# Value sums of attention: the two halves added on VectorE and transposed, instead of one fp32 product with a stacked identity

## The chip, the cores and the metric

One core of a Trainium2 chip runs the whole program. The metric is the device time of one execution in microseconds. It has five engines that run side by side and wait for each other by semaphores: TensorE (PE; its weight loads are shown apart as PEld), VectorE (DVE), ScalarE (ACT), GpSimd (POOL) and SyncE (SP, which issues the DMAs).

## The reference, cut to what matters

The reference is a two-layer diffusion backbone over 1024 latent and 256 context tokens. The change lies in the attention of each layer, which has 10 heads (4 latent-attention heads of key width 96, "MLA"; 6 grouped-query heads of width 64, "GQA"), all with values of width 64:

```python
def block(qi):
    s = jnp.einsum('bkgqd,bksd->bkgqs', qi, k).astype(F32) * scale
    p = jax.nn.softmax(s, axis=-1).astype(v.dtype)
    return jnp.einsum('bkgqs,bkse->bkgqe', p, v)
```

Latent queries see all 1280 keys. In layer 0 the 256 context queries are computed too, and see the 256 context keys only; layer 1 computes latent queries alone.

## The kernel before, in words

Everything is fp32. To multiply faster, an operand is split into a high part (`pth` of the probabilities) that the fast fp32r product takes exactly, and the remainder (`ptl`). The values stand the same way: the stationary tile of a value product (`mvs`, `gvs`) is 128 columns wide, 64 columns of the high part and 64 of the low part. The value sum `O` therefore comes out as two halves, 64 partitions each, that have to be added, and it is feature by token, while the normalisation by the softmax sum wants token by feature.

Work is cut into turns n, one block of 128 queries of one head each: N = 100 in layer 0 (8 latent blocks and then 2 context blocks per head) and N = 80 in layer 1. Two turns make a pair G = n // 2, whose value products go to one PSUM bank `O[G % 2]`. Pairs: 50 in layer 0 and 40 in layer 1. No scheduler is at work: each engine has its instructions in the order in which the code writes them, and waits in that order.

In turn n, PE does this (the loop at L1252): `transposes(n)` of the probabilities into the scores' bank (L1207); in an even turn the high value product of pair n/2 - 1 (L1233), in an odd turn the low one; in an even turn `fold_halves` of pair n/2 - 2 (L1243); then `scores(n + 2)` (L1195), in pieces, each of which waits until `low(n)` on VectorE has read the same piece of the bank (`lo_done`).

VectorE in turn n (L1389): `maximum(n + 1)` (L1345, L1348), `low(n)` (three subtractions, L1363, then one reciprocal, L1367), `first_part(n + 2)`, the maximum over the first 512 scores (L1337), and in an even turn `normalise` of pair n/2 - 2 (L1377).

ScalarE: `high(n)` (L1309), a flush now and then (L1285), `exp(n + 1)` (L1298), and in an odd turn `evacuate` (L1291), which copies the 128 x 256 value sum of pair n // 2 - 1 from PSUM to `osb`.

`fold_halves` multiplies `osb` by `fold`, two 64 x 64 identities on top of each other. This adds the halves and turns them to token by feature in one step. It is an ordinary fp32 product, 2 instructions per pair; the profile lists 2 records for each.

`flush(n)` on PE puts two transposes of finished output (L1218) before the last two blocks of `transposes(n)`, in 5 (layer 0) or 4 (layer 1) successive turns after every second head; 2 of them are even turns.

Of the kernel before, what the change touches and what calls it, by code (L numbers as in the profile page):

```python
# [15 lines left out]
P = 128  # L16
# [34 lines left out]
def backbone(nc, a):  # L51
# [970 lines left out]
    def attention(layer, last, first_head, unit, early, block, ret):  # L1022
# [14 lines left out]
        with Scope() as s:  # L1037
# [9 lines left out]
            negmax, rsum = s.sb("negmax", [P, N]), s.sb("rsum", [P, N])  # L1047
            part_max, rinv = s.sb("part_max", [P, N, 2]), s.sb("rinv", [P, N])
            osb = [s.sb(f"osb{i}", [P, 256]) for i in range(2)]
            fold = s.sb("fold", [P, HD])  # L1050
            o_tok = s.sb("o_tok", [P, BLK, P])
            o_feat = s.sb("o_feat", [P, 2, 256])
            S = [s.ps(f"scores{i}", [P, 3 * 512]) for i in range(2)]
# [3 lines left out]
            s_first, part_done, rest_done = s.sem("s_first"), s.sem("part_done"), s.sem("rest_done")  # L1057
            s_done, max_done, exp_done = s.sem("s_done"), s.sem("max_done"), s.sem("exp_done")
            t_done, hi_done, lo_done = s.sem("t_done"), s.sem("hi_done"), s.sem("lo_done")
            pv_done, osb_done, fold_done, o_done = s.sem("pv_done"), s.sem("osb_done"), s.sem("fold_done"), s.sem("o_done")  # L1060
            own, folder = s.sem("own"), s.sem("folder")
            flush_t, flushed = s.sem("flush_t"), s.sem("flushed")
            stored = [s.sem(f"stored{i}") for i in range(2)]
            early_in, early_hi, early_lo = s.sem("early_in"), s.sem("early_hi"), s.sem("early_lo")
# [108 lines left out]
            def _(pe):  # L1173
# [61 lines left out]
                    if end:  # L1235
                        mm.then_inc(pv_done, 1)

                def fold_halves(G):
                    pe.wait_ge(osb_done, G + 1)
                    if G == 0:  # L1240
                        pe.wait_ge(folder, 1)
                    for j in range(2):
                        mm = nc.tensor.matmul(O[G % 2][:, 256 + j * HD:256 + (j + 1) * HD], osb[G % 2][:, j * P:(j + 1) * P], fold[:, :],  # L1243
                                              start=True, stop=True)
                    mm.then_inc(fold_done, 1)
                scores(0)
                ret.variance(pe, ret.turns - 2)
                ret.outer(pe, ret.turns - 1)
# [3 lines left out]
                for n in range(N + FLUSH0 + NP):  # L1252
                    if n == 0:
                        scores(2)
                        continue
                    if n < N:
                        transposes(n)
                    elif flush_of(n):
                        flush(n)
                    G = n // 2 - 1  # L1260
                    if 0 <= G < NG:
                        if n % 2 == 0:
                            if G >= 2:
                                pe.wait_ge(o_done, G - 1)
                            values(G, pth, hi_done, cut[2 * G + 2], False)
                        else:
                            values(G, ptl, lo_done, cut[2 * G + 2], True)
                    if n % 2 == 0 and 0 <= G - 1 < NG:
                        fold_halves(G - 1)
                    if n + 2 < N:  # L1270
                        scores(n + 2)

# [14 lines left out]
            def evacuate(act, G):  # L1287
                act.wait_ge(pv_done, G + 1)
                if G >= 2:
                    act.wait_ge(fold_done, G - 1)  # L1290
                nc.scalar.activation(osb[G % 2][:, :], O[G % 2][:, :256], ACT.Copy).then_inc(osb_done, 1)  # L1291

            @block.scalar
            def _(act):
# [38 lines left out]
            def _(dve):  # L1333
# [16 lines left out]
                def low(n):  # L1350
                    G, j = n // 2, n % 2
                    if j == 0 and G >= 2:
                        dve.wait_ge(pv_done, G - 1)
                    if n == 2:
                        dve.wait_ge(ret.out_done, ret.turns)
                        for k in range(2):
                            dve.wait_ge(ret.out_stored[k], 16 * (ret.turns // 2))
                    for p, (k0, k1) in enumerate(pieces(n)):
                        dve.wait_ge(hi_done, cut[n] + p + 1)
                        if k0 == 8 and flush_of(n):  # L1360
                            g, f = flush_of(n)
                            dve.wait_ge(flushed, g * NP + f + 1)
                        nc.vector.tensor_tensor(ptl[G % 2][:, k0:k1, j * P:(j + 1) * P],  # L1363
                                                S[n % 2][:, k0 * P:k1 * P].rearrange("p (b q) -> p b q", q=P),
                                                pth[G % 2][:, k0:k1, j * P:(j + 1) * P].bitcast(f32), ALU.subtract).then_inc(lo_done, 1)
                    dve.wait_ge(exp_done, n + 1)
                    nc.vector.reciprocal(rinv[:, n:n + 1], rsum[:, n:n + 1]).then_inc(own, 1)  # L1367

                def normalise(G):
                    n = 2 * G  # L1370
                    g, hd, f = n // NS, head_of(n) % 2, (n % NH) // 2
                    b = block_of(n)
                    dve.wait_ge(fold_done, G + 1)
                    dve.wait_ge(own, n + 2)
                    if g:
                        dve.wait_ge(flush_t, (g - 1) * NP + f + 1)
                    nc.vector.tensor_tensor(o_tok[:, b:b + 2, hd * HD:(hd + 1) * HD],  # L1377
                                            O[G % 2][:, 256:256 + 2 * HD].rearrange("p (j e) -> p j e", e=HD),
                                            rinv[:, n:n + 2].unsqueeze(2).to_broadcast([P, 2, HD]), ALU.mult).then_inc(o_done, 1)
                first_part(0)  # L1380
                maximum(0)
# [2 lines left out]
                first_part(1)  # L1384
                maximum(1)
                ret.finish(dve, ret.turns - 1)
                nc.vector.tensor_tensor(fold[:, :], ident[:, :HD], ident[:, HD:], ALU.add).then_inc(folder, 1)
                first_part(2)
                for n in range(1, N + FLUSH0 + NP):  # L1389
                    if n + 1 < N:  # L1390
                        maximum(n + 1)
                    if n < N:
                        low(n)
                    if n + 2 < N:
                        first_part(n + 2)
                    if n % 2 == 0 and 0 <= n // 2 - 2 < NG:
# [1126 lines left out]
```

## Time and profile before

| what | value |
|---|---|
| median of 3 runs | 3383.92 us (3383.41 to 3385.73) |
| the profiled execution's own time | 3385.56 us |
| its span | 3383.8 us |
| PE busy | 3321.8 us, 98% of the span |
| DVE busy | 2246.2 us, 66% |
| ACT busy | 1252.0 us, 37% |
| attention, layer 0 | about 454 to 827 us of the span |
| attention, layer 1 | about 2228 to 2549 us |

The busy share of an engine counts its instructions, not how well they fill it. Within attention the engines wait for each other inside every turn, so a share over the whole span says little about it; the order of starts in the timeline does.

### The profile page before, as it was taken

To read this page: it belongs to the slowest core of one execution; us is meant where nothing else is said; L and a number is where in the kernel's file an instruction comes from. 1 tells how busy PE (TensorE), PEld (TensorE's weight loads), DVE (VectorE), ACT (ScalarE), POOL (GpSimd) and SP (SyncE) were. 2 spreads that over 40 slices of the span, in tenths; PEclk is the share of its full clock that TensorE was granted. 3 is DMA by queue.
4 is the path that set the end of the run, shared out by engine and by line. 5 is a ranking of instruction groups with operands and counts; after the bars stand their busy time and mean duration, and the time that the engine had idled before them with its cause. 6 is when DMAs were issued, how large, how long until landed. Compare 5 with 4: busy or idle time off the path is not lost. (4 is left out here: it accounts for less than half of the span.)

```text
span 3383.8 us, 48755 instructions
## 1 busy us (share of the span) xinstructions
PE 3321.8 (98%) x17988; PEld 2825.5 (84%) x17988; DVE 2246.2 (66%) x3432; ACT 1252.0 (37%) x2128; POOL 1068.4 (32%) x1121
## 2 busy tenths in 40 slices
PE   8999999999999999999999999999999999999998
PEld 4888888888888888888888788889998788888886
DVE  6575567887178888888756543578992656656566
ACT  4332356776241122112223432366772322222222
POOL 0222310111424444444434122410014344343443
PEclk9999999999999999999999999999999999999999
DMA  6445562222112222222110424462212111111111
GB/s 255 151 184 213 148 197 64 54 71 71 40 56 75 74 74 74 74 80 75 54 39 26 180 103 153 145 199 53 58 43 89 38 55 44 50 50 43 50 44 61
DMA packets 100272, 305.34 MB, mean 90 GB/s; under 512 B 12448, under 2 KB 39200, under 8 KB 97824
## 3 DMA queue, kind: packets, MB, share of 16 engines
q1 hardware_dynamic: 100128, 303.40, 27.6%
q8 instruction: 93, 1.52, 0.2%
q14 instruction: 51, 0.42, 0.0%
HBM read 240.17 MB, written 63.18 MB: 90 GB/s over the span
## 5 line engine op out<-in xcount | busy, mean ns | idle before, releaser
L131 POOL TENSOR_TENSOR wlo<-raw,whi 128x256 fp32r<-128x256 f32 x516 | 494.6, 988 | 814.9 <-ACT whi L119 814.9
L2270 DVE SCALAR_TENSOR_TENSOR xT<-down_acc,mod,xT 128x512 f32<-128x512 f32 (+1 forms) x800 | 496.3, 694 | 236.1 <-PE down_acc L194 234.1
L1993 POOL TENSOR_TENSOR hid_lo<-y,hid_hi 128x256 fp32r<-128x256 f32 (+1 forms) x189 | 185.2, 1011 | 622.5 <-ACT hid_hi L2167 622.5
L2156 ACT ACTIVATE up<-up_acc 128x512 f32<-128x512 f32 (+1 forms) x210 | 115.4, 551 | 580.0 <-PE up_acc L194 579.0
L192 PE MATMUL up_acc<-mix_hi,whi 128*128 128x512 f32 (+1 forms) x875 | 323.6, 370 | 1.8 <-DVE mix_lo L487 0.9
L193 PE MATMUL up_acc<-mix_lo,whi 128*128 128x512 f32 (+1 forms) x875 | 322.5, 369 | 0.0
L194 PE MATMUL up_acc<-mix_hi,wlo 128*128 128x512 f32 (+1 forms) x875 | 322.0, 368 | 0.0
L192 PE MATMUL up_acc<-late_hi,whi 128*128 128x512 f32 (+1 forms) x860 | 316.7, 368 | 0.0
L194 PE MATMUL up_acc<-late_hi,wlo 128*128 128x512 f32 (+1 forms) x860 | 316.4, 368 | 0.0
L193 PE MATMUL up_acc<-late_lo,whi 128*128 128x512 f32 (+1 forms) x860 | 316.4, 368 | 0.0
L192 PE MATMUL down_acc<-hid_hi,first_whi 128*128 128x512 f32 (+1 forms) x825 | 304.6, 369 | 1.4 <-DVE xT L2317 1.4
L193 PE MATMUL down_acc<-hid_lo,first_whi 128*128 128x512 f32 (+1 forms) x825 | 303.3, 368 | 0.0
L194 PE MATMUL down_acc<-hid_hi,first_wlo 128*128 128x512 f32 (+1 forms) x825 | 303.3, 368 | 0.0
L1309 ACT ACTIVATE pth<-scores 128x512 fp32r<-128x512 f32 (+1 forms) x500 | 225.8, 522 | 189.8 <-PE scores L1207 189.8
L1363 DVE TENSOR_TENSOR ptl<-scores,pth 128x512 fp32r<-128x512 f32 (+1 forms) x500 | 267.0, 587 | 20.3 <-ACT pth L1309 19.8
L247 DVE CUSTOM_DVE_ANT_0 mod_product<-norm_buf,silu_all 128x1024 f32<-128x1024 f32 x156 | 234.8, 1505 | 20.4 <-DMA norm_buf<-in_w_ada 11.0
L131 POOL TENSOR_TENSOR first_wlo<-first_raw,first_whi 128x256 fp32r<-128x256 f32 x220 | 210.2, 986 | 113.3 <-ACT first_whi L119 113.3
L119 ACT ACTIVATE first_whi<-first_raw 128x1024 fp32r<-128x1024 f32 x55 | 58.3, 1060 | 465.5 <-PE down_acc L194 391.8
L1298 ACT ACTIVATE probs<-scores,negmax 128x1280 f32<-128x1280 f32 (+1 forms) x180 | 224.7, 1248 | 10.1 <-DVE negmax L1348 10.1
L1207 PE MATMUL scores<-ident,probs 128*128 128x128 f32 x1640 | 216.9, 274 | 5.3 <-ACT probs L1298 5.3
L2249 DVE TENSOR_SCALAR y<-up,convw 128x1284 f32<-128x1284 f32 (+1 forms) x86 | 92.3, 1073 | 189.9 <-ACT up L2156 180.4
L1207 PEld LDWEIGHTS scores<-ident,probs 128*128 128x128 f32 x1640 | 184.7, 141 | 8.4 <-ACT probs L1298 7.8
(329 smaller groups left out, 7501.7 us busy)
## 6 DMA issues: line engine op xcount, KB each, us to landing
raw<-in_w_rest SPq DMA_DIRECT2D x112, 512.0 KB, 3.6
norm_buf<-in_w_ada SPq DMA_DIRECT2D x78, 512.0 KB, 4.5
first_raw<-in_w_rest SPq DMA_DIRECT2D x57, 512.0 KB, 3.6
proj_scratch<-stage SPq DMA_DIRECT2D x18, 640.0 KB, 4.4
raw<-in_w_first SPq DMA_DIRECT2D x21, 512.0 KB, 6.7
ada_raw<-in_w_ada SPq DMA_DIRECT2D x6, 1536.0 KB, 14.5
xT<-proj_scratch SPq DMA_DIRECT2D x4, 1920.0 KB, 8.9
xT<-in_xT SPq DMA_DIRECT2D x8, 640.0 KB, 24.9
```

What stands on the lines that cost most here:

```text
L131: m = nc.gpsimd.tensor_tensor(self.lo[k][:, x:x + 256], self.raw[k][:, x:x + 256], self.hi[k][:, x:x + 256].bitcast(f32), ALU.subtract)
L192: nc.tensor.matmul(out, hi, xhi, start=start, stop=False)
L193: nc.tensor.matmul(out, hi, xlo, start=False, stop=False)
L194: return nc.tensor.matmul(out, lo, xhi, start=False, stop=stop)
L247: nc.vector.tensor_tensor_reduce(product[:, :], self.raw[:, f, :], silu_all[:, :, w], 1.0, 0.0, ALU.mult, ALU.add, self.sums[:, f, w:w + 1 ...
L1207: tr = nc.tensor.transpose(S[n % 2][:, b * P:(b + 1) * P], probs[n % 2][:, b * P:(b + 1) * P], ident[:, :])
L1298: nc.scalar.activation(probs[n % 2][:, :nk], S[n % 2][:, :nk], ACT.Exp, bias=negmax[:, n:n + 1], accum_out=rsum[:, n:n + 1]).then_inc(exp_ ...
L1309: nc.scalar.activation(pth[G % 2][:, k0:k1, j * P:(j + 1) * P], S[n % 2][:, k0 * P:k1 * P].rearrange("p (b q) -> p b q", q=P), ACT.Copy).t ...
L1363: nc.vector.tensor_tensor(ptl[G % 2][:, k0:k1, j * P:(j + 1) * P], S[n % 2][:, k0 * P:k1 * P].rearrange("p (b q) -> p b q", q=P), pth[G % ...
L1993: m = nc.gpsimd.tensor_tensor(hid_lo[:, x:z], y[1][:, x:z], hid_hi[:, x:z].bitcast(f32), ALU.subtract)
L2156: nc.scalar.activation(up[half][:, pc:pc + w], ub[c][:, :w], ACT.Copy).then_inc(up_evac, 1)
L2270: nc.vector.scalar_tensor_tensor(xs, db[g % DB][:, :w], mod_of(layer, 5, m, c), xs, ALU.mult, ALU.add).then_inc(added, 1)
```

## The change

- `evacuate` on ScalarE copies only the lower half (partitions 64 to 127) of the sum, to `lows`, which is 64 partitions of an existing tile (`product`).
- New on VectorE: `add_halves(G)` adds the upper half in PSUM and `lows`, 64 x 256, into `osb`. Its place is behind `low(n)` of the even turn n = 2G + 4, ahead of `first_part(n + 2)`.
- `to_tokens` on PE replaces `fold_halves` at the same place: two 128 x 128 transposes of `osb` with the identity. It waits for `sum_done` from VectorE where `fold_halves` waited for `osb_done` from ScalarE.
- The reciprocals are taken for two blocks at once, in odd turns only.
- Two clearings of the unused half of `osb` replace the addition that made `fold`, once per layer.

```diff
-                def fold_halves(G):
-                    pe.wait_ge(osb_done, G + 1)
+                def to_tokens(G):
+                    pe.wait_ge(sum_done, G + 1)
                     if G == 0:
-                        pe.wait_ge(folder, 1)
+                        pe.wait_ge(zeroed, 1)
                     for j in range(2):
-                        mm = nc.tensor.matmul(O[G % 2][:, 256 + j * HD:256 + (j + 1) * HD], osb[G % 2][:, j * P:(j + 1) * P], fold[:, :],
-                                              start=True, stop=True)
-                    mm.then_inc(fold_done, 1)
+                        tr = nc.tensor.transpose(O[G % 2][:, 256 + j * P:256 + (j + 1) * P], osb[G % 2][:, j * P:(j + 1) * P], ident[:, :])
+                    tr.then_inc(fold_done, 1)
...
-                        fold_halves(G - 1)
+                        to_tokens(G - 1)
...
             def evacuate(act, G):
                 act.wait_ge(pv_done, G + 1)
                 if G >= 2:
-                    act.wait_ge(fold_done, G - 1)
-                nc.scalar.activation(osb[G % 2][:, :], O[G % 2][:, :256], ACT.Copy).then_inc(osb_done, 1)
+                    act.wait_ge(sum_done, G - 1)
+                nc.scalar.activation(lows[G % 2], O[G % 2][HD:, :256], ACT.Copy).then_inc(low_out, 1)
...
-                    dve.wait_ge(exp_done, n + 1)
-                    nc.vector.reciprocal(rinv[:, n:n + 1], rsum[:, n:n + 1]).then_inc(own, 1)
+                    if j == 1:
+                        dve.wait_ge(exp_done, n + 1)
+                        nc.vector.reciprocal(rinv[:, n - 1:n + 1], rsum[:, n - 1:n + 1]).then_inc(own, 1)
+
+                def add_halves(G):
+                    dve.wait_ge(low_out, G + 1)
+                    if G >= 2:
+                        dve.wait_ge(fold_done, G - 1)
+                    nc.vector.tensor_tensor(osb[G % 2][:HD, :], O[G % 2][:HD, :256], lows[G % 2], ALU.add).then_inc(sum_done, 1)
...
                     if n < N:
                         low(n)
+                    if n % 2 == 0 and 0 <= n // 2 - 2 < NG:
+                        add_halves(n // 2 - 2)
                     if n + 2 < N:
                         first_part(n + 2)
```

The order of instructions at the first pair, with what each waits for. On VectorE, even turn 4 of layer 0, before: the three subtractions of `low`, the reciprocal, then the first part of the maximum of turn 6.

```order
L1363 TENSOR_TENSOR ptl_209<-scores_223,pth_210 128x4x128 [waits hi_done_241,pv_done_243]
L1363 TENSOR_TENSOR ptl_209<-scores_223,pth_210 128x4x128 [waits hi_done_241]
L1363 TENSOR_TENSOR ptl_209<-scores_223,pth_210 128x2x128 [waits hi_done_241]
L1367 RECIPROCAL rinv<-rsum 128x1 [waits exp_done_239]
L1337 TENSOR_REDUCE part_max<-scores_223 128x1 [waits s_first_234]
```

The same place now:

```order
L1362 TENSOR_TENSOR ptl_209<-scores_222,pth_210 128x4x128 [waits hi_done_240,pv_done_242]
L1362 TENSOR_TENSOR ptl_209<-scores_222,pth_210 128x4x128 [waits hi_done_240]
L1362 TENSOR_TENSOR ptl_209<-scores_222,pth_210 128x2x128 [waits hi_done_240]
L1373 TENSOR_TENSOR osb_218<-values_224,mod_product 64x256 [waits low_out_243]
L1336 TENSOR_REDUCE part_max<-scores_222 128x1 [waits s_first_233]
```

The addition of 64 x 256 has taken the reciprocal's place, and stands behind all three subtractions of the turn.

On PE, the same even turn before: the transposes of turn 4, the high value product of pair 1, the fold of pair 0, the first scores of turn 6.

```order
L1207 MATMUL scores_223<-ident,probs_212 128x128 [waits exp_done_239]
L1207 MATMUL scores_223<-ident,probs_212 128x128 x9
L1233 MATMUL values_226<-pth_208,mix_hi 128x256 [waits hi_done_241]
L1233 MATMUL values_226<-pth_208,mix_hi 128x256 x9
L1243 MATMUL values_225<-fold,osb_218 128x64 [waits folder_248,osb_done_244]
L1243 MATMUL values_225<-fold,osb_218 128x64
L1195 MATMUL scores_223<-first_kh,first_qh 128x512 [waits lo_done_242]
```

And now:

```order
L1207 MATMUL scores_222<-ident,probs_212 128x128 [waits exp_done_238]
L1207 MATMUL scores_222<-ident,probs_212 128x128 x9
L1233 MATMUL values_225<-pth_208,mix_hi 128x256 [waits hi_done_240]
L1233 MATMUL values_225<-pth_208,mix_hi 128x256 x9
L1243 MATMUL values_224<-ident,osb_218 128x128 [waits zeroed_248,sum_done_244]
L1243 MATMUL values_224<-ident,osb_218 128x128
L1195 MATMUL scores_222<-first_kh,first_qh 128x512 [waits lo_done_241]
```

Nothing has moved on PE. The instruction ahead of the scores now waits for VectorE's `sum_done`, which comes from the addition shown above, instead of ScalarE's `osb_done`.

## Rows read from the trace of the kernel before

**Rows 1.** Page, part 1: busy time, share and instructions of each engine.

```profile
PE 3321.8 (98%) x17988; PEld 2825.5 (84%) x17988; DVE 2246.2 (66%) x3432; ACT 1252.0 (37%) x2128; POOL 1068.4 (32%) x1121
```

**Rows 2.** Groups by shape, DVE, 454 to 830 us: busy us, mean ns, idle before.

```profile
L1363 DVE TENSOR_TENSOR ptl<-scores,pth 128x256 fp32r<-128x256 f32 x100 | 41.5, 415 | 3.7 <-ACT pth L1309 3.7
L1377 DVE TENSOR_TENSOR o_tok<-values,rinv 128x128 f32<-128x128 f32 x50 | 14.0, 281 | 3.1 <-PE values L1243 3.1
```

**Rows 3.** Timeline, layer 1, GQA, even turn: start, duration us, [idle before, releaser].

```profile
2401.57 0.40 ACT L1291 ACTIVATE osb<-values 128x256 f32<-128x256 f32 x1
...
2401.98 1.25 PE L1207 MATMUL scores<-ident,probs 128*128 128x128 f32 x10
...
2403.38 1.62 DVE L1363 TENSOR_TENSOR ptl<-scores,pth 128x512 fp32r<-128x512 f32 x3
...
2404.14 0.53 PEld L1243 LDWEIGHTS values<-fold,osb 128*128 128x128 f32 x4
...
2404.59 0.19 PEld L1195 LDWEIGHTS scores<-ks,qh 128*128 128x128 f32 x1
...
2404.91 0.15 DVE L1367 RECIPROCAL rinv<-rsum 128x1 f32<-128x1 f32 x1
...
2405.37 0.69 DVE L1337 TENSOR_REDUCE part_max<-scores 128x1 f32<-128x512 f32 x1 [0.30 <-PE scores L1195]
```

**Rows 4.** Timeline, layer 0, MLA, even turn with full blocks on both sides.

```profile
513.60 0.30 PEld L1195 LDWEIGHTS scores<-mix_lo,qh 96*128 96x128 f32 x2
...
513.92 0.15 DVE L1367 RECIPROCAL rinv<-rsum 128x1 f32<-128x1 f32 x1
```

**Rows 5.** Timeline, layer 0, MLA, even turn that begins a head.

```profile
505.22 0.30 PEld L1195 LDWEIGHTS scores<-mix_lo,qh 96*128 96x128 f32 x2 [0.40 <-DVE ptl L1363]
...
506.01 0.15 DVE L1367 RECIPROCAL rinv<-rsum 128x1 f32<-128x1 f32 x1
```

**Rows 6.** Timeline, layer 0, GQA, even turn that begins a head.

```profile
655.04 1.62 DVE L1363 TENSOR_TENSOR ptl<-scores,pth 128x512 fp32r<-128x512 f32 x3
...
655.78 0.19 PEld L1195 LDWEIGHTS scores<-ks,qh 128*128 128x128 f32 x1 [0.40 <-DVE ptl L1363]
...
656.58 0.15 DVE L1367 RECIPROCAL rinv<-rsum 128x1 f32<-128x1 f32 x1
```

**Rows 7.** Timeline, layer 0, MLA, last full even turn of a head, context next.

```profile
492.33 0.19 PEld L1195 LDWEIGHTS scores<-first_kh,first_qh 96*128 96x128 f32 x1
...
492.64 0.15 DVE L1367 RECIPROCAL rinv<-rsum 128x1 f32<-128x1 f32 x1
...
493.12 1.07 PEld L1207 LDWEIGHTS scores<-ident,probs 128*128 128x128 f32 x10 [0.37 <-ACT probs L1298]
```

**Rows 8.** Timeline, layer 0, MLA, even context turn.

```profile
497.13 0.15 DVE L1367 RECIPROCAL rinv<-rsum 128x1 f32<-128x1 f32 x1
...
497.56 0.30 PEld L1195 LDWEIGHTS scores<-mix_lo,qh 96*128 96x128 f32 x2
```

**Rows 9.** Timeline, layer 0, GQA: the two transposes of a flush.

```profile
633.84 0.25 PEld L1218 LDWEIGHTS scores<-ident,o_tok 128*128 128x128 f32 x2
```

**Rows 10.** Who waited, line 1195's scores for `ptl`: us in total, times.

```profile
PEld scores L1195: 28.5, 65
```

**Rows 11.** Busy by window: length, PE, PEld, DVE, ACT, POOL, granted clock, DMA, GB/s.

```profile
468.00:471.40 3.40, 3.23 (x9) 2.65 (x10) 1.80 (x5) 1.35 (x3) 0.00 (x0) 0.51 0.99 351
```

**Rows 12.** Timeline of PE alone, third turn of layer 0, and of layer 1.

```profile
465.99 1.31 PE L1207 MATMUL scores<-ident,probs 128*128 128x128 f32 x10 [1.03 <-ACT probs L1298]
468.17 0.80 PE L1195 MATMUL scores<-first_kh,first_qh 96*128 96x512 f32 x1 [0.87 <-DVE ptl L1363]
...
475.42 0.40 PE L1195 MATMUL scores<-first_kh,first_qh 96*128 96x512 f32 x1
...
479.45 0.40 PE L1195 MATMUL scores<-first_kh,first_qh 96*128 96x512 f32 x1
...
2235.29 0.50 PE L1195 MATMUL scores<-first_kh,first_qh 96*128 96x512 f32 x1 [0.86 <-DVE ptl L1363]
```

More of the change, by code:

```diff
@@ L1049, in attention @@
             osb = [s.sb(f"osb{i}", [P, 256]) for i in range(2)]
-            fold = s.sb("fold", [P, HD])
+            lows = [product[0:HD, i * 256:(i + 1) * 256] for i in range(2)]
             o_tok = s.sb("o_tok", [P, BLK, P])
@@ L1059, in attention @@
             t_done, hi_done, lo_done = s.sem("t_done"), s.sem("hi_done"), s.sem("lo_done")
-            pv_done, osb_done, fold_done, o_done = s.sem("pv_done"), s.sem("osb_done"), s.sem("fold_done"), s.sem("o_done")
-            own, folder = s.sem("own"), s.sem("folder")
+            pv_done, low_out, sum_done, fold_done, o_done = (s.sem(x) for x in ("pv_done", "low_out", "sum_done", "fold_done", "o_done"))
+            own, zeroed = s.sem("own"), s.sem("zeroed")
             flush_t, flushed = s.sem("flush_t"), s.sem("flushed")
@@ L1373, in normalise @@
                     dve.wait_ge(fold_done, G + 1)
-                    dve.wait_ge(own, n + 2)
+                    dve.wait_ge(own, G + 1)
                     if g:
@@ L1377, in normalise @@
                     nc.vector.tensor_tensor(o_tok[:, b:b + 2, hd * HD:(hd + 1) * HD],
-                                            O[G % 2][:, 256:256 + 2 * HD].rearrange("p (j e) -> p j e", e=HD),
+                                            O[G % 2][:, 256:].rearrange("p (j e) -> p j e", e=P)[:, :, :HD],
                                             rinv[:, n:n + 2].unsqueeze(2).to_broadcast([P, 2, HD]), ALU.mult).then_inc(o_done, 1)
@@ L1386, in _ @@
                 ret.finish(dve, ret.turns - 1)
-                nc.vector.tensor_tensor(fold[:, :], ident[:, :HD], ident[:, HD:], ALU.add).then_inc(folder, 1)
+                for b in osb:
+                    zero = nc.vector.memset(b[HD:, :], 0.0)
+                zero.then_inc(zeroed, 1)
                 first_part(2)
```

## The prediction

> **What bounds the kernel now.** I read the page first: PE is busy for 98% of the span [rows 1], so time is either PE's own work or a wait put in front of it. The fold is PE work, and lies in attention alone, so the rest of the reading is the timeline there, one pair at a time.
>
> Take an even turn of layer 1 [rows 3]. PE transposes (2401.98), makes the high value product, loads for the fold (2404.14), and goes straight on to the next scores (2404.59). The fold costs PE 0.45 us, and waits for nothing: the copy to `osb` had ended at 2401.97, over 2 us before. VectorE runs the three subtractions of `low` from 2403.38; the reciprocal's start at 2404.91 marks their end. What the reader is to see is that PE begins the next scores 0.32 us before VectorE has finished `low`. That is allowed because scores go piece by piece behind it. VectorE's next maximum then sits idle for 0.30 us until PE's scores are there. So in an even turn PE is ahead, and VectorE follows it.
>
> **The change part by part.** *PE.* The fold's 0.45 us go. Two transposes of 128 x 128 come. The two of a flush show a load time of 0.25 us for two loads of 0.14 us [rows 9], so they start 0.11 us apart and PE is through with two in some 0.21 us. Saved: 0.24 us per pair, over 90 pairs 22 us, if nothing else moved.
>
> The Trainium skill (Perfetto Trace Analysis, Transposes) says to do logical transposes in transpose mode and not as a standard matmul. The trace agrees on PE's own price, 0.21 against 0.45 us; by that rule alone the sum would be -22 us. It does not speak of what the transposes have to wait for.
>
> *VectorE.* The addition of 64 x 256 with one operand in PSUM has no row. The nearest is the 128 x 256 subtraction with one operand in PSUM, 0.415 us [rows 2]; the columns are the same, and I take 0.42. From below it is bounded by the 128-column multiplication from PSUM, 0.28 us [rows 2], from above by the 512-column reduction, 0.69 us [rows 3]. The even turn's reciprocal, 0.15 us, goes; the addition starts in its place. In odd turns the reciprocal of two columns costs what that of one did.
>
> *ScalarE.* Copying 64 partitions instead of 128 with the same columns stays at some 0.40 us [rows 3]; that copy ends far ahead either way. If it got slower by a microsecond it would still be hidden behind `high` and `exp`. The two clearings and the missing `fold` are a few tenths per layer, behind the first turns.
>
> *The wait that is added.* This is the main term. `to_tokens` waits for the addition, which stands behind all of `low(n)` of the same even turn. Behind `to_tokens` on PE are queued the scores of turn n + 2, then everything. So these scores lose their piecewise start: they can begin only at the time where the reciprocal started, plus 0.42 (addition), plus 0.05 (from VectorE's end to PE's load, read where the first subtraction, 655.04 and 0.69 long, released the load at 655.78 [rows 6]), plus 0.21 (transposes), in all 0.68 us after the row of the reciprocal. Applied place by place:
>
> - Full blocks on both sides. GQA: 2404.91 + 0.68 = 2405.59 against 2404.59 [rows 3], +1.00. MLA: 513.92 + 0.68 = 514.60 against 513.60 [rows 4], +1.00. In turns with a flush PE reaches the place 0.22 us later anyway [rows 9] and `low` does not, so +0.78. Layer 0 has 19 such pairs (4 with a flush), layer 1 has 37 (8 with a flush). Without flush 44 x 1.00 = 44.0; with it 12 x 0.78 = 9.4.
> - The even turn that begins a head in layer 0, 9 times. The value product is of a context pair and short, so PE is early and waited for the first piece already. 506.01 + 0.68 = 506.69 against 505.22 [rows 5], +1.47; GQA 656.58 + 0.68 = 657.26 against 655.78 [rows 6], +1.48. 9 x 1.47 = 13.2.
> - The last full even turn of a head, 10 times. The scores are of a context block and short, and PE then waited 0.37 us for the exponential [rows 7]. The scores took from 492.33 to 493.12 - 0.37 = 492.75, so 0.42. Now 492.64 + 0.68 + 0.42 = 493.74 against 493.12, +0.62; with a flush (4) +0.40. Sum 5.3.
> - The even context turn, 9 times with scores behind it: 497.13 + 0.68 = 497.81 against 497.56 [rows 8], +0.25. Sum 2.3.
> - First and last pairs of both layers, where no scores follow: some 0.5 in all.
>
> Does a later wait swallow the shift? The transposes of turn n + 1 follow the scores on PE directly. VectorE's maximum of turn n + 2 already waited for those scores [rows 3], so it moves by the same amount, and `low(n + 1)` with it. The waits of the odd turns hang on a chain that itself starts at the shifted scores, so I let nothing be swallowed. DMAs are far ahead and get more time.
>
> Sum: 44.0 + 9.4 + 13.2 + 5.3 + 2.3 + 0.5 = 74.7 us. This is made on the profiled execution, span 3383.8 (own time 3385.56, inside the spread of the three runs); the median is 3383.92. Forecast 3383.9 + 74.7 = 3458.6 us, slower by 2.2%.
>
> **The rivals.** *The clock falls as well.* In the third turn of layer 0 PE ran nothing but ten transposes from 464.96 (465.99 less its idle 1.03) to 468.17 [rows 12]; the granted clock in the window behind it was 0.51, the 1.2 GHz level [rows 11]. From these scores to the next took 7.25 us, where the full clock gave 4.03 (475.42 to 479.45) [rows 12]: a fall costs 3.2 us. The same gap in layer 1 (scores at 2235.29 after the same waits) did not make it fall. With the change the beginning of a head looks alike: ten transposes, two short value products, and 2 us of waiting. If the clock falls at all 9, the time is 3458.6 + 29 = 3487 us. For it: one of two such gaps fell. Against it: here a little real work lies inside. Chance 0.2, and a fall at all the other pairs too (56 x 3.2 = 179 more, near 3670 us) 0.03; there a whole high value product of ten matmuls lies between.
> The Trainium skill (TensorE: Matmul & The Clock Gate, Part 4: PE-mode transpose) says that transposes do not count as PE being busy for the clock. By that rule, the gap of layer 0 [rows 12], filled with transposes alone, agrees; the like gap in layer 1 passed at full clock and does not bear it out.
>
> *The shift is partly swallowed.* PE waited for `ptl` ahead of scores 65 times, 28.5 us in all [rows 10]. If the shifts used all of it up, the sum is 74.7 - 28.5 = 46 us, 3430 us. Against it is the argument above. Chance 0.08.
>
> *The other side: PE's saving shows and the addition is hidden.* VectorE would have to hand over the sum before PE has ended its high value product; the point where this decides is `low` ending 0.47 us before PE arrives. Then the time is 3383.9 - 22 = 3362 us. The skill's rule on transposes named above gives this. Against it: the subtractions end 0.77 us after PE gets there (2404.91 against 2404.14) [rows 3]. Chance 0.03. That the two effects meet within measurement: 0.02.
>
> **How the numbers follow.** Forecast 0.64, clock at the heads' beginnings 0.2, clock everywhere 0.03, swallowed 0.08, faster 0.03, none 0.02. The unknown duration of the addition acts on about 84 places: at 0.28 us the sum falls by 12 (3447), at 0.69 us it rises by 23 (3481). The likeliest case's own range is 3446 to 3475; with the clock's rival above the range is 3444 to 3488 us. A measurement of this kernel tells 0.2% (7 us) from no change; faster has 0.03, the same 0.02, slower 0.95.
>
> **What would show it.** In the profile after: `to_tokens` (L1243) released by VectorE's `osb` addition at nearly every pair, with a wait of about 0.8 us; its two transposes 0.11 us apart; the addition at 0.42 us, starting where the reciprocal did; the idle of VectorE before the first maximum (L1336) of even turns as before or longer; the distance from one even turn to the next grown by 1.0 us; attention longer by some 39 us in layer 0 and 36 in layer 1, all else unmoved; and the clock near 1.00 except where a head begins, if the rival holds. The forecast is wrong if the pair's period grows by much less than a microsecond although the wait is there: then something on the chain had slack that I did not see. It is wrong upward if the clock's row shows half speed inside attention.

## The result and the profile after

The changed kernel takes 3462.21 us (median of 4 runs, 3459.87 to 3466.85) against 3383.66 us (4 runs, 3383.28 to 3385.73) for the kernel before on the same chip: the ratio is 1.0233, with an interval of 1.0215 to 1.025. It is slower by 78.6 us, where 74.7 us were forecast. The profiled execution took 3459.87 us with a span of 3458.0 us; against the span before of 3383.8 us that is 74.2 us more.

The page's first part, which answers to [rows 1]:

```profile
PE 3320.4 (96%) x17808; PEld 2809.1 (81%) x17808; DVE 2273.3 (66%) x3434; ACT 1260.4 (36%) x2128; POOL 1071.5 (31%) x1121
```

PE does 1.4 us less work than before in a span 74 us longer, so nearly all of the loss is time in which PE stands idle. Where it stands is in the view of line 1243 (durations in ns, then the idle time before it in us and how often):

```profile
L1243 PEld LDWEIGHTS values<-ident,osb x180: 137/141/145, 481.1 to 2621.5; 128*128 128x128 f32 x180
L1243 PE MATMUL values<-ident,osb x180: 271/273/332, 481.1 to 2621.6; 128*128 128x128 f32 x180
...
  DVE osb L1373: 184.1, 178
```

The 184.1 us count two rows for each wait. The view of who waited for whom keeps the loads and the matmuls apart (total us, times, longest us); below its first line stand the two other waits around it:

```profile
PEld values L1243 <- DVE osb L1373: 101.1, 89, 2.1
DVE part_max L1336 <- PE scores L1195: 94.0, 106, 1.8
...
PEld scores L1195 <- DVE ptl L1362: 23.1, 51, 1.7
```

Before the change the fold waited for VectorE nowhere. Now 89 of 90 pairs wait, for 101.1 / 89 = 1.14 us on average. VectorE in turn waits longer at its next maximum (94.0 us, where the same view of before has 49.9), because PE's scores come later, and the scores' own wait for `ptl` falls only from 28.5 us [rows 10] to 23.1.

The timeline of the turn of [rows 3], now 58 us later:

```profile
2459.36 0.38 ACT L1290 ACTIVATE mod_product<-values 64x256 f32<-64x256 f32 x1
...
2459.60 1.25 PE L1207 MATMUL scores<-ident,probs 128*128 128x128 f32 x10
...
2461.00 1.62 DVE L1362 TENSOR_TENSOR ptl<-scores,pth 128x512 fp32r<-128x512 f32 x3
...
2462.53 0.41 DVE L1373 TENSOR_TENSOR osb<-values,mod_product 64x256 f32<-64x256 f32 x1
...
2462.99 0.20 PEld L1243 LDWEIGHTS values<-ident,osb 128*128 128x128 f32 x2 [1.15 <-DVE osb L1373]
...
2463.16 0.19 PEld L1195 LDWEIGHTS scores<-ks,qh 128*128 128x128 f32 x1
...
2463.93 0.69 DVE L1336 TENSOR_REDUCE part_max<-scores 128x1 f32<-128x512 f32 x1 [0.99 <-PE scores L1195]
```

ScalarE's copy of the lower half has ended at 2459.74, and the sums of the upper half are there as long. The addition starts only at 2462.53, behind the three subtractions of a later turn. PE's loads have run out at about 2461.84 (2462.99 - 1.15), its matmuls 0.2 us later, and PE stands until the addition has ended. From the transposes of `probs` to the next scores it is 3.56 us (2459.60 to 2463.16), before it was 2.61 us (2401.98 to 2404.59) [rows 3]: 0.95 us lost in this pair.

At the beginning of a head in layer 0 the wait is the longest. The turn of [rows 5]:

```profile
501.23 1.25 PE L1207 MATMUL scores<-ident,probs 128*128 128x128 f32 x10
...
502.24 0.48 PE L1233 MATMUL values<-pth,mix_hi 128*128 128x256 f32 x2
...
504.17 0.41 DVE L1373 TENSOR_TENSOR osb<-values,mod_product 64x256 f32<-64x256 f32 x1
...
504.62 0.20 PEld L1243 LDWEIGHTS values<-ident,osb 128*128 128x128 f32 x2 [2.11 <-DVE osb L1373]
504.79 0.30 PEld L1195 LDWEIGHTS scores<-mix_lo,qh 96*128 96x128 f32 x2
```

PE's idle of 2.11 us is followed by a fall of the granted clock, that is a stretch of some microseconds at the lower of its two levels. Busy time by window behind four heads' beginnings (length, PE, PEld, DVE, ACT, POOL, granted clock, DMA share, GB/s):

```profile
504.00:508.00 4.00, 3.37 (x15) 3.04 (x16) 2.07 (x5) 0.59 (x2) 0.00 (x0) 0.75 0.93 210
592.00:596.00 4.00, 4.00 (x20) 3.44 (x18) 2.15 (x5) 0.79 (x2) 0.00 (x0) 0.65 0.02 4
673.00:677.00 4.00, 4.00 (x19) 3.65 (x18) 2.53 (x5) 0.90 (x2) 1.79 (x2) 0.57 0.32 125
752.00:756.00 4.00, 4.00 (x18) 3.60 (x17) 3.36 (x9) 2.27 (x4) 1.84 (x2) 0.60 0.31 127
```

The granted clock 0.57 in a window means that most of it ran at the 1.2 GHz level. PE looks fully busy there and did less: the last three windows hold 18 to 20 of its matmuls, and those of before at about the same times (592:596, 672:676, 752:756) 29 to 32. Before, the clock was 1.00 at all nine places where a head begins. In this execution it fell at four of them.

### The profile page after: what moved, and what is told of

Read it like the earlier page. It is cut to its first block and busy times, and to the rows that moved or that the text cites. A ratio compares the mean times of both kernels' runs of the same rounds, so it can differ in the third digit from the quotient of the medians.

```text
span 3458.0 us, 48483 instructions
## 1 busy us (share of the span) xinstructions
PE 3320.4 (96%) x17808; PEld 2809.1 (81%) x17808; DVE 2273.3 (66%) x3434; ACT 1260.4 (36%) x2128; POOL 1071.5 (31%) x1121
## 5 line engine op out<-in xcount | busy, mean ns | idle before, releaser
L192 PEld LDWEIGHTS up_acc<-mix_hi,whi 128*128 128x128 f32 x875 | 165.0, 189 | 31.9 <-issue 3.3
```

The costliest lines, as they stand in the source:

```text
L192: nc.tensor.matmul(out, hi, xhi, start=start, stop=False)
```

## The experiments

Each kernel was timed beside the kernel before. That one measured 3383.05 us in the company of the first four experiments, 3383.18 us with the next four, and 3383.6 us with the last two; each time its runs lay within 3382.2 and 3386. "Per pair" is the growth of the distance from the transposes of one even turn to those of the next turn, read in the two traces; where the odd turn behind it changes too, that is said.

**1. The addition ahead of the subtractions.** If the wait comes from the addition's place on VectorE, moving it by one call takes the loss away.

```
-                    if n < N:
-                        low(n)
                     if n % 2 == 0 and 0 <= n // 2 - 2 < NG:
                         add_halves(n // 2 - 2)
+                    if n < N:
+                        low(n)
```

> One line moved on VectorE against the changed kernel: the addition of the halves stands ahead of the even turn's three subtractions instead of behind them; everything it adds is still there. If the place of the addition in VectorE's order, with PE's scores queued behind the transposes, is the cause (my theory), PE finds the sum ready when its high value product ends, the wait of about 0.8 us per pair goes, and only the subtractions start 0.35 us later: nearly all of the 78 us go, and with the cheaper PE part the time is 3370 to 3385 us. If the added VectorE work itself is the cost (rival: VectorE is the bound, 0.25 us more per pair), at least 20 us stay wherever it stands: 3405 us or more. If the clock's falls are the main cost, the time follows them: they would go too only if PE's waits go.

Measured: 3379.62 us (3377.65 to 3380.37), ratio 0.9989 (0.998 to 0.9999). The whole 79 us are gone, with the same instructions in another order. Its timeline in layer 1:

```profile
2399.56 0.42 DVE L1373 TENSOR_TENSOR osb<-values,mod_product 64x256 f32<-64x256 f32 x1
2399.90 1.60 DVE L1362 TENSOR_TENSOR ptl<-scores,pth 128x512 fp32r<-128x512 f32 x3
...
2400.38 0.24 PEld L1243 LDWEIGHTS values<-ident,osb 128*128 128x128 f32 x2
...
2400.63 0.19 PEld L1195 LDWEIGHTS scores<-ks,qh 128*128 128x128 f32 x1
...
2401.22 0.19 PEld L1195 LDWEIGHTS scores<-ks,qh 128*128 128x128 f32 x1 [0.30 <-DVE ptl L1362]
```

The transposes wait for nothing. The subtractions start after the addition, and PE's second piece of scores waits for them (0.30 us): what is saved on PE is given back here. Per pair of full blocks MLA gains 0.11 to 0.25 us, mostly 0.17. GQA gains 0.05 in the even turn and 0.10 in the odd one behind it, and 0.23 where a flush lies. The beginning of a head loses 0.30, but for the second (0.04 gained). So VectorE's 0.41 us cost something in this place too, but far less.

**2. The transposes behind the scores.** The same knot, untied from the other side: the addition stays where it is, and PE does the next scores first.

```
-                    if n % 2 == 0 and 0 <= G - 1 < NG:
-                        to_tokens(G - 1)
                     if n + 2 < N:
                         scores(n + 2)
+                    if n % 2 == 0 and 0 <= G - 1 < NG:
+                        to_tokens(G - 1)
```

> One line moved on PE against the changed kernel: the two transposes of the summed halves stand behind the scores of turn n + 2 instead of ahead of them; VectorE's order is that of the changed kernel. If the cost is what is queued behind PE's wait (my theory), it goes although the addition still stands behind the subtractions: 3375 to 3395 us, a little above the experiment with the addition moved, since the normalisation now waits for PE's scores and delays VectorE's next maximum by some 0.1 to 0.3 us in the GQA heads. If the added VectorE work is the cost, 3405 us or more.

Measured: 3388.76 us (3386.0 to 3390.61), ratio 1.0015 (1.0005 to 1.0024). Of the 79 us 5.7 are left, although the addition is still behind `low`. The wait thus costs only through what is queued behind it on PE. What is left does not lie in the even turns of full blocks, which gain 0.12 to 0.24 us each but for two. VectorE's normalisation now waits for the transposes:

```profile
DVE o_tok L1383 <- PE values L1243: 24.4, 54, 0.6
```

The odd turns behind lose some 0.10 us each (4.7 in all) and the beginnings of a head 3.2 us together, and a fall of the clock at the start of layer 1 (behind 2241 us) takes another 1.6.

**3. The transposes alone.** The kernel before, with the product by `fold` replaced by transposes of the whole `osb`; there is no addition, so the low halves are left out of the result. The normalisation reads the columns where they now stand.

```
-                        mm = nc.tensor.matmul(O[G % 2][:, 256 + j * HD:256 + (j + 1) * HD], osb[G % 2][:, j * P:(j + 1) * P], fold[:, :],
-                                              start=True, stop=True)
+                        mm = nc.tensor.transpose(O[G % 2][:, 256 + j * P:256 + (j + 1) * P], osb[G % 2][:, j * P:(j + 1) * P], ident[:, :])
```

> The PE part alone, on the kernel before: ScalarE still copies all 128 partitions, PE transposes them in transpose mode instead of the product with the stacked identity, nothing is added on VectorE (the low halves are left out of the output), and PE waits for ScalarE as before. If the transposes save PE 0.24 us per pair as the rows say and PE's order carries it on, the time falls by up to 22 us in the MLA heads and less in the GQA heads where VectorE sets the pace: 3362 to 3376 us. If two transposes cost PE as much as the product (rival), 3383 us; slower than 3390 us would mean that the transposes themselves hurt, by the clock for example.

Measured: 3367.09 us (3366.7 to 3367.57), ratio 0.9952 (0.9935 to 0.9969). PE's saving is real: 0.22 to 0.24 us per pair of full blocks, MLA and GQA alike, and as much in the context turns. It is 0 where a head begins and in the last full turn, where PE was waiting anyway. That makes some 65 x 0.23 = 15 us. The profiled execution is 18.1 us shorter than the one before the change; the other 3.1 us are a fall of the clock in the first turns of layer 0 [rows 12] that it does not have. The rule of the Trainium skill (Perfetto Trace Analysis, Transposes) to use transpose mode for a logical transpose agrees with this run.

**4. The addition alone.** The changed kernel, with an fp32 product by the identity's first 64 columns in place of the transposes; the normalisation reads its columns accordingly.

```
-                        tr = nc.tensor.transpose(O[G % 2][:, 256 + j * P:256 + (j + 1) * P], osb[G % 2][:, j * P:(j + 1) * P], ident[:, :])
+                        tr = nc.tensor.matmul(O[G % 2][:, 256 + j * HD:256 + (j + 1) * HD], osb[G % 2][:, j * P:(j + 1) * P], ident[:, :HD],
+                                              start=True, stop=True)
```

> The addition alone, on the changed kernel: everything as changed, but the summed halves are turned to tokens by a fp32 product with 64 columns of the identity, as costly on PE as the one before. If the wait is the cost, the changed kernel's time plus 0.24 us for each of about 84 pairs whose scores are behind it: 3462 + 20 = 3482 us (3475 to 3488). If the transposes had a part in the loss, it is below 3462 us. The clock may help here: ordinary products stand where transposes stood, so fewer falls than 5 in attention if transposes do not count for it.

Measured: 3491.04 us (3489.81 to 3492.86), ratio 1.0318 (1.03 to 1.0335), above the upper end expected. Per pair it loses 1.22 us, 0.27 more than the changed kernel, as it should. With the last full turns, the context turns and the beginnings of a head that makes 23 of the 33 us between the two profiled executions. Most of the rest is the clock. It fell at six beginnings of a head, where the changed kernel's profile has four (3.0 us more), and in the first turns of layer 0 and of layer 1 (behind 468 and 2294 us), where that one has none (3.0 us each). Both have one more just behind layer 0's attention (884 and 864 us). Three of the six:

```profile
642.00:646.00 4.00, 4.00 (x19) 3.63 (x19) 2.00 (x4) 0.51 (x1) 0.00 (x0) 0.57 0.00 0
...
724.00:728.00 4.00, 4.00 (x17) 3.61 (x18) 1.77 (x3) 0.10 (x1) 0.00 (x0) 0.57 0.02 6
806.00:810.00 4.00, 4.00 (x18) 3.56 (x16) 3.38 (x7) 1.95 (x4) 0.00 (x0) 0.57 0.02 4
```

**5. The addition twice.** If `to_tokens` hangs on VectorE's chain alone, one more addition ahead of it moves every pair by its duration.

```
+                    nc.vector.tensor_tensor(product[0:HD, 512 + G % 2 * 256:768 + G % 2 * 256], O[G % 2][:HD, :256], lows[G % 2], ALU.add)
                     nc.vector.tensor_tensor(osb[G % 2][:HD, :], O[G % 2][:HD, :256], lows[G % 2], ALU.add).then_inc(sum_done, 1)
```

> The changed kernel with the addition made twice on VectorE in the same place (the first into columns that nobody reads). If every tenth of a microsecond in front of to_tokens goes straight into the period (my theory), each of some 88 places gets 0.35 us more: 3462 + 31 = 3493 us (3487 to 3500). If something later in the turn has slack, clearly less.

Measured: 3495.22 us (2 runs, 3491.69 and 3498.75), ratio 1.0331 (1.0312 to 1.035).

```profile
2487.80 0.41 DVE L1373 TENSOR_TENSOR mod_product<-values,mod_product 64x256 f32<-64x256 f32 x1
2488.13 0.41 DVE L1374 TENSOR_TENSOR osb<-values,mod_product 64x256 f32<-64x256 f32 x1
```

The two start 0.33 us apart, and the pairs' loss goes from 0.95 to 1.28 us, by just as much. No slack lies on the chain. In this run too the clock fell behind some beginnings of a head (640, 681, 722 and 804 us).

**6. GpSimd adds.** ScalarE copies both halves, and GpSimd, which had room, adds them in SBUF between its own splits. VectorE is rid of the addition.

```
+                nc.scalar.activation(ups[G % 2], O[G % 2][:HD, :256], ACT.Copy).then_inc(low_out, 1)
...
+                for G in range(NG):
+                    pool.wait_ge(low_out, 2 * G + 2)
...
+                    nc.gpsimd.tensor_tensor(osb[G % 2][:HD, :], ups[G % 2], lows[G % 2], ALU.add).then_inc(sum_done, 1)
+                    for _ in range(2):
+                        if steps and (steps[0][0] <= G):
+                            _, f, args = steps.pop(0)
+                            f(*args)
```

> The changed kernel with the addition taken off VectorE: ScalarE copies both halves out of PSUM (two copies of 64 x 256, 0.4 us more per pair, in time in which it waited for PE), GpSimd adds them in SBUF (64 x 256, about 1 us, interleaved with the splits that it makes in the later heads), PE transposes as changed and waits for GpSimd, and no instruction of VectorE stands in front. By my theory the sum is ready before PE asks for it, nothing waits, and PE's saving of 0.22 us per pair is all that is left: as with the transposes alone, 3364 to 3373 us, faster than both kernels. If the wait only changes its name (rival: GpSimd comes later than the high value product ends), 3390 us or more.

Measured: 3378.08 us (3375.49 to 3383.71), ratio 0.9984 (0.9975 to 0.9994): the best that computes everything, but 5 us above the range expected.

```profile
2398.81 0.38 ACT L1312 ACTIVATE mod_product<-values 64x256 f32<-64x256 f32 x1
...
2399.22 0.38 ACT L1313 ACTIVATE mod_product<-values 64x256 f32<-64x256 f32 x1
...
2399.67 0.72 POOL L1186 TENSOR_TENSOR osb<-mod_product 64x256 f32<-64x256 f32 x1 [4.72 <-ACT mod_product L1313]
...
2401.23 0.24 PEld L1265 LDWEIGHTS values<-ident,osb 128*128 128x128 f32 x2
```

GpSimd's sum is there at 2400.39, PE wants it at 2401.23. Full pairs gain 0.22 us as in experiment 3. What is missing lies elsewhere. The two profiled executions are 12.8 us apart. Of these, 8.4 us lie where the clock fell and did not in experiment 3: in the first turns of layer 0 (behind 469 us, 3.7), between the layers (823 us, 2.5) and in the first turns of layer 1 (2237 us, 2.2). The first and the last of these hold 0.6 us each that is not the clock's but belongs to the two clearings (see the terms of the sum below). The context turns are 2.0 us longer, where most of the waits for GpSimd lie (8.6 us in 16 turns in all), and the end of layer 1 is 1.9 us longer, with PE's wait of 1.66 us for GpSimd's last sum.

**7. PE filled at the heads' beginnings.** Ten idle matmuls of 256 columns behind the short context product, in layer 0 only, into a part of PSUM that the transposes overwrite. They lie inside the wait, so they cost nothing, unless the falls of the clock come from PE's idle time; then they save those.

```
                             values(G, pth, hi_done, cut[2 * G + 2], False)
+                            if is_ctx(2 * G) and n < N:
+                                h = head_of(2 * G)
+                                for k in range(10):
+                                    nc.tensor.matmul(O[G % 2][:, 256:], mvs[:, k % 2, h, :] if is_mla(h) else gvs[:, k % 2, h % 2, :],
+                                                     pth[G % 2][:, k % 2, :], start=False, stop=False)
```

> The changed kernel with ten more matmuls of 256 columns on PE in the even turn that begins a head in layer 0 (behind the two of the context pair, into columns of the bank that the transposes overwrite later), in the time in which PE waits for the sum. They take about 1.27 us of a wait of 1.9 us and delay nothing. If the clock's falls in the changed kernel (5 in layer 0's attention, 3.4 us each) come from that gap, they become rarer or stop, and each is worth 1.3 us: 3452 to 3459 us with a granted clock above that of the changed kernel. If the falls have nothing to do with it: 3462 us and as many falls.

Measured: 3458.32 us (3457.64 to 3460.29), ratio 1.0223 (1.0207 to 1.0238), 3.9 us below the changed kernel, whose runs were on another chip. The ten matmuls cost nothing: a head's beginning takes as long as in the changed kernel where the clock held.

**8. The wait alone.** The kernel before, with its product by `fold`, made to wait for `low(n)` of the same turn; no addition and no transposes.

```
                     if n % 2 == 0 and 0 <= G - 1 < NG:
+                        if n < N:
+                            pe.wait_ge(lo_done, cut[n + 1])
                         fold_halves(G - 1)
```

> The kernel before with one wait more and nothing else: PE waits for the last subtraction of the even turn ahead of the fold. No addition, the fp32 product and the copy on ScalarE as before. If the order is the cost and not the work, most of the loss is there without any addition: the scores start at the reciprocal's row plus 0.57 us (0.07 to the end of the subtractions, 0.05, the fold's 0.45) instead of 0.68, so about 0.89 us per full pair, 65 us in all and 3440 to 3458 us. If the addition's work is the cost, 3384 us.

Measured: 3450.66 us (2 runs, 3450.39 and 3450.93), ratio 1.0199 (1.018 to 1.0218): 67 us, without any of the change's arithmetic. The timeline:

```profile
2453.25 1.62 DVE L1365 TENSOR_TENSOR ptl<-scores,pth 128x512 fp32r<-128x512 f32 x3
...
2454.79 0.15 DVE L1369 RECIPROCAL rinv<-rsum 128x1 f32<-128x1 f32 x1
2454.92 0.52 PEld L1243 LDWEIGHTS values<-fold,osb 128*128 128x128 f32 x4 [0.84 <-DVE ptl L1365]
...
2455.36 0.19 PEld L1195 LDWEIGHTS scores<-ks,qh 128*128 128x128 f32 x1
```

**9 and 10. The changed kernel and the filled one, side by side.** The changed kernel had not been timed beside the filled one, and 3.9 us is little against its spread. So both ran again together, unaltered.

> The changed kernel unaltered, beside the filled one on the same chip: 3458 to 3466 us, with 2 to 6 falls of the clock in attention, at the beginnings of heads in layer 0.

> The filled kernel again on the same chip. If the ten matmuls at each head's beginning keep the clock up, no fall at those places and 3 to 7 us less than the changed kernel beside it; if the first look was chance, the two agree and falls are there.

Measured: the changed kernel 3465.62 us (3460.4 to 3467.12), the filled one 3456.41 us (3455.05 to 3457.98), 9.2 us less, where 3 to 7 were expected; the ranges do not touch. Windows of the changed kernel, behind three heads' beginnings:

```profile
508.00:512.00 4.00, 4.00 (x19) 3.67 (x18) 2.23 (x5) 0.72 (x2) 0.00 (x0) 0.57 1.01 227
552.00:556.00 4.00, 4.00 (x19) 3.88 (x18) 3.03 (x6) 1.57 (x4) 0.00 (x0) 0.57 0.00 0
675.00:679.00 4.00, 4.00 (x19) 3.66 (x19) 2.35 (x5) 0.73 (x2) 0.53 (x1) 0.57 0.53 164
```

And of the filled one, where in this run and in that of experiment 7 the clock fell at none of the nine beginnings:

```profile
508.00:512.00 4.00, 3.42 (x23) 2.95 (x22) 3.32 (x7) 2.10 (x4) 0.00 (x0) 1.00 0.95 228
592.00:596.00 4.00, 3.46 (x23) 3.05 (x23) 2.50 (x7) 1.30 (x4) 0.00 (x0) 1.00 0.00 0
672.00:676.00 4.00, 2.94 (x20) 2.55 (x20) 2.89 (x7) 1.89 (x5) 0.04 (x1) 1.00 0.49 168
```

The two profiled executions are 5.6 us apart: 4.5 at the beginnings of a head, and 1.3 between the layers, where the changed kernel has a fall at 867 us, just behind attention, that the filled one lacks. Whether the filling has a part in that one is open; in experiment 7 the clock fell there (860 us). The executions that make the rest of the 9.2 us have no profile.

## Why the prediction was right, step by step

**The wait is the cost, and its place on VectorE the cause.** This was the main term, and the runs show it from four sides: the wait alone gives 67 us (experiment 8), moving the addition ahead of `low` gives them back (1), moving the transposes out from in front of the scores does too (2), and a second addition adds its own 0.33 us to each pair (5). Predicted was that the scores load 0.68 us after the place of the reciprocal. It is 0.63 (2462.53 to 2463.16): the addition 0.41 instead of 0.42, the hand-over 0.05 as read, and the two transposes 0.17 (2462.99 to 2463.16) instead of 0.21. One of the signs was misjudged: the wait was put at about 0.8 us and is 1.15, near what the forecast's own terms give (2404.91 + 0.42 + 0.05 - 2404.14 = 1.24).

**The terms of the sum**, from the starts of the transposes in the traces, places with the clock at 1.00 (for the beginnings of a head, experiment 10 has all nine):

| place | forecast | measured |
| --- | --- | --- |
| 44 full pairs | 1.00 each, 44.0 | 0.95, 41.8 |
| 12 with a flush | 0.78, 9.4 | 0.73, 8.8 |
| 9 beginnings of a head | 1.47, 13.2 | 1.37 GQA, 1.43 MLA but 1.09 at its middle one, 12.1 |
| 10 last full turns | 0.62 and 0.40, 5.3 | 0.51 and 0.24 MLA, 0.40 and 0.12 GQA, 3.3 |
| 9 context turns | 0.25, 2.3 | 0.18 to 0.20, once 0.54, 2.1 |

The 0.05 us that each pair lacks is that of the step above, and at two of the three MLA beginnings nothing else is missing (1.47 less 0.05 is 1.42). At the middle one the kernel before already began its scores 0.3 us later than the forecast's row has it (0.72 us of waiting for `ptl` where [rows 5] shows 0.40). At the beginning of a GQA head more is missing. In the trace of before the scores that loaded at 655.78 [rows 6] were held up once more by a piece of `ptl`, and it took 1.30 us until the next transposes loaded; after the change they run in one go in 1.17 us (690.96 to 692.13, next GQA head). The forecast moved the first piece and forgot that the later pieces gain; of 1.43 us (1.48 less 0.05) 1.30 are left, and 0.07 come in the turn behind. The full pairs showed no such gain, since there the pieces flowed already. The last full turns were sized from one MLA row without a flush [rows 7]; the GQA ones lose 0.40 and 0.12, and this is the largest miss among the small terms, 2.0 us.

**PE's own saving** was put at 0.24 us per pair, and is 0.22 to 0.24 (experiment 3). But 22 us for 90 pairs, and with it the 3362 us of the rival on the other side, was too much: where PE waits anyway the saving vanishes, and transposes alone reach 3367 us.

**The clearings** were put at a few tenths per layer, inside the 0.5 us for the first and last pairs. They cost 0.6 us in the second turn of each layer. The two clearings take VectorE 0.55 us (2272.24 to 2272.79), where the addition for `fold` took 0.22; the maximum behind them starts 0.35 us after PE's transposes (2272.82, 2272.47), before it was 0.28 us ahead of them (2232.83, 2233.11). Of the nine profiled executions with the clearings seven show 0.63 to 0.66 us in that turn of layer 1 (in the other two the clock fell there), and experiments 3 and 8, which have none, show 0.00 and -0.02.

**Almost nothing was swallowed.** Odd turns without a fall of the clock or its neighbourhood differ by 0.00 to 0.08 us, but for the second turn of each layer (above) and two in layer 1 (0.24 and 0.34 us), whose cause was not looked for. Only the GQA beginnings of a head gave a little back. Attention grew from 362.6 to 400.4 us in layer 0 and from 314.4 to 349.3 in layer 1, by 37.8 and 34.9, where 39 and 36 were forecast. The rival of 3430 us is out, and with it the one that nothing changes.

**The clock's rival came true in part**, and this the forecast had as an either-or. It gave a fall at all nine beginnings 0.2 and priced it at 3.2 us each, 3487 us. The falls come at some of them: at four in the profiled run (506, 591, 673 and 752 us), at others in experiment 9 (508, 552, 675 and 754). And each costs less. Over the turn and the one behind it the four lost 2.50, 2.93, 2.71 and 2.34 us; against 1.43 (MLA) or 1.37 (GQA) at full clock, a fall costs 1.0 to 1.5 us, 1.2 on average (0.8 to 1.4 in experiment 9). The price of 3.2 us was taken from one place [rows 12], where the records show a longer stretch at half speed than at any of the four. There it was right: experiment 3, which changes nothing else in these turns, lacks that fall and takes 3.1 us less. The changed kernel's profiled execution lacks it too (2.45 us less, the 0.6 of the clearings included). Experiments 7, 9 and 10 show that the falls at the heads' beginnings belong to PE's idle time there: filled, they are gone, and the time is 3.9 and 9.2 us lower.

**So why 78.6 and not 74.7?** The five terms at full clock come to 68.1 us where 74.2 were forecast; this is the part of the sum that was mis-sized (2.8 in the full pairs, 2.0 in the last full turns, 1.1 at the beginnings of a head). In the profiled run the four falls add 4.9, and the first turns of layer 0 take 2.45 off. Some 2.1 us more lie in attention: 0.6 for the clearings in layer 1, 0.04 in each turn behind a last full one, and four single delays of 0.2 to 0.35. That makes 72.7 in attention. The 1.5 us outside it are falls again: one at 386 us before attention is missing (1.1 less), and between the layers stand two, behind 864 and 2202 us, that the kernel before does not have (2.6 more). 74.2 in all. So the profiled run met the forecast partly by luck: the terms fell short by 6 us, and the net of the falls gained and lost, with small delays, made that up. How many falls there are changes from run to run: the mean granted clock of three of the four runs of the changed kernel is 0.995 at 3459.87 us, 0.994 at 3461.54 and 0.992 at 3466.85. The median is thus not a time of the schedule alone.

**What stays open** is why the clock falls at one beginning of a head and not at the next. The Trainium skill (TensorE: Matmul & The Clock Gate, Part 4: PE-mode transpose) would have it that transposes do not count as PE being busy in the same way. Experiment 4 has ordinary products in place of the two added transposes and fell at six beginnings of a head, not four; experiment 8 has no added transposes and fell at two beginnings (550 and 673 us). The two added transposes are therefore not needed for a fall. The ten transposes of `probs` ahead of the wait were in every kernel, and no run replaced them. The gap that the forecast took as its example speaks against any simple rule: in the third turn of layer 0 the clock fell in 9 of the 12 profiled executions (not in the changed kernel's first, nor in experiments 3 and 7), and in the like gap of layer 1 in 4 of 12 (experiments 2, 4, 6 and 7). That it passed there at full clock in the kernel before was one draw and no property of the place. Not tested either is that the fast product takes the high part of an operand exactly; that is how the kernel is built.

**A version that beats both** is the one with GpSimd's addition, 3378.08 us, 0.16% below the kernel before (interval 0.06 to 0.25%); the one with the addition ahead of `low`, 3379.62 us, is next and is one moved call. Neither comes near the 3367 us of the transposes alone. Part of that distance is the addition, for which something waits at some places in both. Part is luck with the clock: experiment 3's profile lacks the early fall, which is worth 3.1 us, and theirs have it.

## What to carry to other kernels

When the producer of an operand moves to another engine, its own duration is the small part: look at what stands ahead of it in that engine's order, and at what is queued behind the instruction that will wait. Here 0.41 us of addition cost 0.95 us per pair in one place and almost nothing one call earlier. An operation that saves time on the bounding engine is worth it only where that engine does not wait anyway, so count the places and not the instructions. And where a change leaves the bounding engine idle for two microseconds again and again, look at the granted clock behind each such place, for the idle time can cost a second time.

## What the runs showed of the hardware

- The granted clock fell to the 1.2 GHz level behind waits of PE of about 2 us (2.11 us at the MLA head above), at some of nine like places. The same kernel fell at different places in two executions, and its runs spread over 7 us, the slower ones with the lower mean clock.
- Work that nobody needs made the kernel faster: ten matmuls of 256 columns in each of nine gaps, 3465.62 to 3456.41 us.
- GpSimd adds 64 x 256 fp32 from SBUF in 0.72 us, VectorE with one operand in PSUM in 0.41; two such additions on VectorE start 0.33 us apart, so a second one cost less than its duration.
- ScalarE's copy from PSUM takes 0.38 us for 64 partitions and 0.40 for 128 [rows 3]: half the partitions save next to nothing.
- Two transposes of 128 x 128 fp32 with a load of 0.14 us each hold PE's loads for 0.17 us; the products that they replaced, with four loads, for 0.45 [rows 3].
